# A ten-buffer gather, spills on GpSimd and ScalarE one-hots in the U stage of a hybrid decoder layer; norms that scale the rows

## The reference, cut to what matters

```
q   = (h @ wq).reshape(B, S, 8, 2, 128)
sub = einsum("bshpd,hpnd->bshpn", q, keys)
sv, si = top_k(sub, 16)                      # per half, then 16 of the 16*16 sums
experts, gates = ids of the best 16, softmax(best)
act = gelu(einsum("cd,ced->ce", xb, u_tab[experts]))   # 128 experts a token
out = einsum("ce,ced->cd", gates * act, v_tab[experts])
x = rms_norm(x + out)
```

## Time and profile before

| | us |
|---|---|
| runs, median | 1961.11 |
| lowest, highest of three | 1956.55, 1967.15 |
| profiled execution, its own time | 1952.49 |
| its span, first to last instruction | 1950.7 |
| TensorE busy | 1862.3 (95%) |
| VectorE, ScalarE, GpSimd busy | 1580.6, 1031.1, 783.9 |

### The profile page before, as it was taken

How to read it: one execution, slowest core, us unless ns; L and a number is a source line. 1 busy time by engine, 2 the same in 40 slices (tenths; PEclk the granted TensorE clock), 3 DMA queues, 4 the chain that set the end, 5 groups by cost and what they waited for, 6 DMA issues and landing times.

```text
span 1950.7 us, 34571 instructions
## 1 busy us (share of the span) xinstructions
PE 1862.3 (95%) x13106; PEld 1628.1 (83%) x13106; DVE 1580.6 (81%) x2510; ACT 1031.1 (53%) x1868; POOL 783.9 (40%) x686
## 2 busy tenths in 40 slices
PE   8999999999999999999998989988999999999997
PEld 7888887787889888788887877868999999998886
DVE  6768575676534999899987878878988999999998
ACT  5535454474555454666745656535674444444444
POOL 0000000000011113677635677004776777787773
PEclk9999999999999999999999999999999999999999
DMA  7523333246799997888868989977979999999997
GB/s 251 190 86 131 99 99 109 78 133 226 251 302 310 315 321 221 248 265 268 250 216 279 317 283 314 317 249 258 314 246 372 380 387 383 383 393 392 396 382 265
DMA packets 214741, 520.70 MB, mean 267 GB/s; under 512 B 25424, under 2 KB 98416, under 8 KB 214320
## 3 DMA queue, kind: packets, MB, share of 16 engines
q1 hardware_dynamic: 171952, 356.41, 52.9%
q0 software_dynamic: 42624, 162.08, 24.3%
HBM read 472.18 MB, written 46.20 MB: 266 GB/s over the span
## 4 chain that ended last, share of the span: by engine, by line
PE 60%; DMA 14%; DVE 14%; ACT 5%; issue 4%; POOL 3%; SPq 0%; DVEq 0%; ACTq 0%; POOLq 0%
PE ps L2043 59%; DVE lo L1330 4%; DMA raw<-in_peer_u 3%; DMA vraw<-in_peer_v 3%; DMA oneJ_spill<-hspace 2%; DMA hspace<-u_rows,row_ids 1%; POOL u_early L789 1%; PE ps L2447 1%; DMA u_late<-u_rows,row_ids 1%; ACT hi L870 1%; DMA u_early<-u_rows,row_ids 1%; POOL hspace L789 1%; POOL u_late L789 1%; DVE hspace L1862 1%; DMA oneI<-oneI_spill 1%
## 5 line engine op out<-in xcount | busy, mean ns | idle before, releaser
L2043 PE MATMUL ps<-hT,hi 128*128 128x512 f32 x2736 | 990.4, 405 | 39.1 <-DVE lo L1330 38.8
L2043 PE MATMUL ps<-hT,lo 128*128 128x256 f32 x2736 | 769.1, 281 | 0.0
L2043 PEld LDWEIGHTS ps<-hT,hi 128*128 128x128 f32 x2736 | 517.6, 189 | 176.3 <-issue 33.7
L870 ACT ACTIVATE hi<-raw 128x896 fp32r<-128x896 f32 (+1 forms) x406 | 397.2, 991 | 363.8 <-DMA raw<-in_peer_u 303.5
L1330 DVE TENSOR_TENSOR lo<-raw,hi 128x896 fp32r<-128x896 f32 (+1 forms) x406 | 457.6, 1139 | 126.8 <-ACT hi L870 122.5
L2043 PEld LDWEIGHTS ps<-hT,lo 128*128 128x128 f32 x2736 | 520.4, 190 | 0.1
L827 POOL DMA_INDIRECT got<-in_peer_v,row_ids x256 | 345.9, 1351 | 121.9 <-DVE sums L1338 100.9
L1203 ACT ACTIVATE vhi<-vraw 128x896 fp32r<-128x896 f32 (+1 forms) x256 | 193.6, 765 | 255.4 <-DMA vraw<-in_peer_v 247.7
L2043 PE MATMUL ps<-vhi,a_hi 128*128 128x448 f32 x768 | 242.0, 370 | 7.3 <-DVE vlo L1894 5.6
L1338 DVE SCALAR_TENSOR_TENSOR sums<-got,wT,sums 128x704 f32<-128x704 f32 x256 | 243.0, 949 | 1.4 <-DMA got<-in_peer_v,row_ids 0.9
L2043 PE MATMUL ps<-vlo,a_hi 128*128 128x448 f32 x768 | 241.0, 368 | 0.0
(11 more groups left out here) (314 smaller groups left out, 2257.2 us busy)
## 6 DMA issues: line engine op xcount, KB each, us to landing
raw<-in_peer_u SPq DMA_DIRECT2D x256, 448.0 KB, 4.8
vraw<-in_peer_v SPq DMA_DIRECT2D x124, 448.0 KB, 7.9
raw<-in_w_in SPq DMA_DIRECT2D x86, 512.0 KB, 3.4
vraw<-in_peer_v SPq DMA_DIRECT2D x124, 224.0 KB, 8.0
raw<-in_w_out SPq DMA_DIRECT2D x32, 512.0 KB, 3.8
raw<-in_wq SPq DMA_DIRECT2D x32, 512.0 KB, 5.3
turn_in<-in_peer_u SPq DMA_DIRECT2D x32, 512.0 KB, 5.9
u_rows<-turned POOLq DMA_DIRECT2D x32, 512.0 KB, 5.7
```

The costliest lines, as they stand in the source:

```text
L870: nc.scalar.activation(hi[n % NR][:, 0:w], raw[n % NR][:, 0:w], ACT.Copy).then_inc(hi_done, 1)
L2043: return nc.tensor.matmul(o, lhsT, rhs, start=start, stop=stop, skip_group_check=True)
```

## The change

It consists of these parts.

- Gathered rows: ten buffers in each half (`u_space`: `h0`, `h1` and `e0` to `e7` first, then `l0` to `l3` and `m0` to `m3`, six in all for dots from tile 98 on, four from tile 107 on). `u_buffers` gives each pair its buffer and the pair that had it before. GpSimd waits for the dot (not the sum) of pair k - 6, for the sum of the pair before in the same buffer, and at a first use of an `m` buffer for ScalarE's copies of both `idx` banks.
- Sums: ScalarE sums a dot three pieces behind it (`SUM_LAG`), after the single hi piece.
- Spills: they leave SyncE's queue. GpSimd takes gathers and spills from one order, `pool_order`: a gather of k is keyed by the dot of k - 6 plus 0.6 piece, a spill by its one-hot plus 0.7. The last ones, from `U_LATE`, follow in their order.
- Late one-hots: they begin when the last dot is done, and every second J part is made by ScalarE (`late_j`) as 1 - |j - number| through Abs, four times 128x128, and Relu, 128x512, in one buffer `tail4`. It waits for the landing of the spill two before. VectorE still makes all I parts and the other J parts, with `hspace`.
- The plan: pace 0.92 for 0.87, a late J of ScalarE costs half, the last dot has to stand before tile 113.
- Norms: VectorE scales the rows themselves, four tensor_scalar of 128x512 a half (`rows_scaled`), and TensorE transposes them. In the second norm the additions of the second half are moved among the steps of the first half's factor.
- `w65_ready` and `scan_done` become one semaphore.

What `u_plan` and `pool_order` give (positions as tile, .5 is its second piece):

| | before | after |
|---|---|---|
| room | 1.28 | 1.24 |
| row numbers of the halves | 24.0, 70.0 | 25.0, 72.5 |
| dots 0, 60, 64, 127 | 26.0, 61.5, 72.0, 109.5 | 27.0, 63.5, 74.5, 112.5 |
| idx copied by ScalarE in iteration | 74 | 76 |
| one-hots 0, 31, 63 | 75.0, 107.0, 126.5 | 77.0, 110.5, 126.0 |
| `U_LATE`, its place | 47, 117.5 | 34, 113.5 |
| spills ahead of gather 127 in GpSimd's order | 0 | 30 (0 to 29) |

The diff, without renamed lines and without what only moves:

```diff
@@ u_plan
-        pace = min(pace + 0.87, 2.0)
+        pace = min(pace + 0.92, 2.0)
...
-                ones, credit = ones + 1, credit - ONE_US
+                if late is None and dots == N_PAIR and n > last_dot + 1:
+                    late = ones
+                by_act = late is not None and (ones - late) % 2
+                ones, credit = ones + 1, credit - (ONE_US / 2 if by_act else ONE_US)
...
-    if _done:
+    if _done and LAST_DOT < 2 * (T_U + 113):
@@
+def pool_order():
+    order, key = [], 0.0
+    for k in range(N_PAIR):
+        key = max(key, ROWS_AT[k * NT2 // N_PAIR], DOT_AT[k - U_BUF] + 0.6 if k >= U_BUF else 0)
+        order.append((key, k, "gather"))
+    order += [(ONE_AT[g] + 0.7, g, "spill") for g in range(U_LATE)]
+    return sorted(order)
@@ sync: spill(g) and its calls removed
@@ gpsimd
+            def spill(g):
+                split = g >= U_LATE and (g - U_LATE) % 2 == 0
+                if g < U_LATE or split:
+                    pool.wait_ge(sem("madeJ"), g + 1 if g < U_LATE else U_LATE + (g - U_LATE) // 2 + 1)
+                else:
+                    pool.wait_ge(sem("lateJ_made"), (g - U_LATE) // 2 + 2)
+                pool.dma_start(oneJ_dram[g]..., made_j(g)).then_inc(sem(f"oneJ_out{g % 3}"), 16)
+                pool.wait_ge(sem("madeI"), g + 1)
+                pool.dma_start(oneI_dram[g]..., made_i(g)).then_inc(sem(f"oneI_out{g % 2}"), 16)
@@ gather of pair k
                 if k >= U_BUF:
-                    pool.wait_ge(sem("dots_summed"), k - U_BUF + 1)
+                    pool.wait_ge(sem("dots_made"), k - U_BUF + 1)
+                if U_PREV[k] is not None:
+                    pool.wait_ge(sem("dots_summed"), U_PREV[k] + 1)
+                elif U_HOME[k][0] == "m":
+                    for i in range(2):
+                        wait_read(pool, "idx", i)
@@ scalar
+            def late_j(g):
+                act.wait_ge(sem("p_made"), 1)
+                if g == U_LATE + 1:
+                    act.wait_ge(sem("dots_summed"), N_PAIR)
+                    act.wait_ge(sem("lateJ_made"), 1)
+                else:
+                    act.wait_ge(sem(f"oneJ_out{(g - 2) % 3}"), 16 * ((g - 2) // 3 + 1))
+                for c in range(TOK4):
+                    at_c = TOK4 * (g - U_LATE) + c
+                    ins = nc.scalar.activation(made_j(g)[:, c], iota[:, :], ACT.Abs,
+                                               bias=minus_j[:, at_c:at_c + 1])
+                ins.then_inc(sem("far_made"), 1)
+                act.wait_ge(sem("far_made"), (g - U_LATE) // 2 + 1)
+                nc.scalar.activation(made_j(g), made_j(g), ACT.Relu, scale=-1.0, bias=one_c).then_inc(
+                    sem("lateJ_made"), 1)
...
+                for n in range(2 * (T_U + i) + 2, 2 * (T_U + i) + 4):
+                    if n < 2 * T_V:
+                        hi_piece(n)
+                    for what, k in U_STEPS.get(n - SUM_LAG, []):
+                        if what == "dot":
+                            dots_sum(k)
+                    for what, g in U_STEPS.get(n - 1, []):
+                        if what == "one" and g >= U_LATE and (g - U_LATE) % 2:
+                            late_j(g)
@@ vector, first norm
-                ts(diag[t][:, :], ident[:, :], rs[:, t:t + 1], None, ALU.mult).then_inc(
-                    sem("diag_done"), 1)
+                for q in range(4):
+                    rows = x_sb[:, t, 512 * q:512 * q + 512]
+                    ts(rows, rows, rs[:, t:t + 1], None, ALU.mult).then_inc(sem("rows_scaled"), 1)
@@ vector, second norm
-            add_rows(0, range(4))
-            norm_rows(0)
-            add_rows(1, range(4))
-            norm_rows(1)
+            add_rows(0, range(4))
+            add_rows(1, range(1))
+            norm_sum(0)
+            add_rows(1, range(1, 2))
+            norm_factor(0)
+            add_rows(1, range(2, 4))
+            scale_rows(0)
+            norm_sum(1)
+            norm_factor(1)
+            scale_rows(1)
@@ tensor, first norm (second alike)
-                        ins = mm(bank("x1", j)[...], x_sb[:, t, kc * P:(kc + 1) * P], diag[t][:, :], ...)
+                        ins = nc.tensor.transpose(bank("x1", j)[...],
+                                                  x_sb[:, t, kc * P:(kc + 1) * P], ident[:, :])
```

More of the change, by code:

```diff
@@ L150, with u_buffers @@
     U_STEPS, _done, (U_EXP, U_FIRST, LAST_DOT, ROWS_AT) = u_plan(_room / 100)
-    if _done:
+    if _done and LAST_DOT < 2 * (T_U + 113):
         break
[L153 to L157, removed]
 ONE_AT = {_i: _n for _n in U_STEPS for _what, _i in U_STEPS[_n] if _what == "one"}
-U_LATE = min([_i for _i, _n in ONE_AT.items() if _n >= 2 * (T_U + 117)] + [SEQ // 4])
+DOT_AT = {_i: _n for _n in U_STEPS for _what, _i in U_STEPS[_n] if _what == "dot"}
+U_LATE = min([_i for _i, _n in ONE_AT.items() if _n > LAST_DOT + 1] + [SEQ // 4])
 U_PDOT = LAST_DOT // 2 - T_U + 3
+N_LATE_ACT = (SEQ // 4 - U_LATE) // 2
+SUM_LAG = 3
+def u_buffers():
+    homes, prev, last, half = {}, {}, {}, N_PAIR // 2
+    turn = [0, 0, 0]
+    for k in range(N_PAIR):
+        if k < half:
+            home = (["h0", "h1"] + [f"e{i}" for i in range(8)])[turn[0] % 10]
+            turn[0] += 1
+        elif DOT_AT[k] < 2 * (T_U + 98):
+            home = (["h0", "h1"] + [f"l{i}" for i in range(4)] + [f"m{i}" for i in range(4)])[turn[1] % 10]
+            turn[1] += 1
+        else:
+            late = DOT_AT[k] >= 2 * (T_U + 107)
+            home = (["h0", "h1", "l2", "l3"] + ([] if late else ["l0", "l1"]))[turn[2] % (4 if late else 6)]
+            turn[2] += 1
+        homes[k], prev[k] = home, last.get(home)
+        last[home] = k
+    return homes, prev
+U_HOME, U_PREV = u_buffers()
+def pool_order():
+    order, key = [], 0.0
+    for k in range(N_PAIR):
+        key = max(key, ROWS_AT[k * NT2 // N_PAIR], DOT_AT[k - U_BUF] + 0.6 if k >= U_BUF else 0)
+        order.append((key, k, "gather"))
+    order += [(ONE_AT[g] + 0.7, g, "spill") for g in range(U_LATE)]
+    return sorted(order)
 DD = 1344
@@ L452, in u_got @@
         def u_got(k):
[L454 to L457, removed]
+            home = U_HOME[k]
+            if home[0] == "h":
+                return hspace[:, int(home[1]), 7:KC:8, :]
+            return u_space[home][:, :, :]
         def made_j(g):
@@ L643, in _ @@
                         raw_in[n % NR], 16)
-                    if n - 3 in U_STEPS:
-                        for what, g in U_STEPS[n - 3]:
-                            if what == "one":
-                                spill(g)
                 if t + 1 in U_TURN:
@@ L651, in _ @@
                     load_unit(N_Q)
-            for n in range(2 * T_V - 3, 2 * T_V):
-                for what, g in U_STEPS[n]:
-                    if what == "one":
-                        spill(g)
             def load_v(k):
@@ L793, in _ @@
                         sem(f"got_in{k % U_BUF}"), 16)
+            for _, i, what in pool_order():
+                if what == "gather":
+                    gather_rows(i)
+                else:
+                    spill(i)
+            for g in range(U_LATE, N_TOK4):
+                spill(g)
             def cast_rows(c):
@@ L1194, in _ @@
                         freed("idx", 1), 1)
+                    act.wait_ge(freed("idx", 1), PLAN["idx", 1][1] + 1)
+                    nc.scalar.activation(minus_j[:, :], idxT[:, 1, TOK4 * U_LATE:SEQ], ACT.Copy,
+                                         scale=-1.0).then_inc(sem("lateJ_made"), 1)
             def v_hi(k):
```

96 lines of the change are left out of this document (39 added, 57 removed).

## The result

The changed kernel takes 2002.51 us (median of 4 runs, 1995.82 to 2009.70) where the kernel before takes 1959.86 beside it: ratio 1.0198, 95% interval 1.0150 to 1.0245. I had forecast 1968, with a range to 1985: the time lies outside it. The profiled execution took 1995.8 us, with a span of 1994.0 where before has 1950.7; 43.3 us are to be explained, where my sum has 7.

What follows compares the result with a forecast made beforehand. TensorE, busy 95% of the span, was taken as the bound, so changes pay only where it starves. First dots -8.5, second dots +7, tail +8.5 and norms 0 gave 7 us slower: 1968 us, range 1945 to 1985.

Steps and rivals of the forecast that it cites:

- my sum: Whole kernel: the four steps added up, 7 us slower; chance 0.40, own range 1959 to 1975 us.
- Norms, nothing: Both norms: row scaling by VectorE and transposes by TensorE change the time by 0 us.
- First dots, -8.5: First dots of the U stage: GpSimd's waits for sums go, 8.5 of 10.5 us lost are gained.
- Second dots, +7: Second dots of the U stage: spills on GpSimd's queue make it set the pace, 7 us more lost.
- 198 us to spill 29: Second dots: GpSimd's time for 56 pairs and 30 spills before issuing spill 29, which VectorE's one-hot 31 awaits.
- Tail, +8.5: Tail of the U stage: ScalarE waits for J spills to land, 19.6 us lost for 11.1.
- The round: Tail: ScalarE's four Abs, Relu and wait for its J spill's landing, 5.5 us, fourteen times.
- Cheap gathers: Rival, dots: gather issues fall to a mean of about 1.0 us, kernel faster at 1943 us; chance 0.22.
- A J landing of 2.5 or of 4.3: Two rivals, tail: spill lands in 2.5 us, total 1960, chance 0.14; or in 4.3, total 1985, chance 0.14.
- Cold transposes: Rival, norms: transposes don't bring TensorE's doubled pace, so products start at half pace, 1974 us; chance 0.08.
- The chance of 0.30 for slower: Whole kernel: probability given to a result more than 0.5% slower; faster had 0.27, within 0.5% 0.43.
- Theory G: Experiments' forecasts, first dots: unbroken trains of gathers keep TensorE short of instructions; four pairs open saves 4 to 10 us.

Runs made afterwards that it cites:

- 10: Changed kernel with at most four pairs of gathers open instead of six; ratio 1.0122 to the kernel before.
- run 11: Changed kernel with spills issued by SyncE and at most four pairs of gathers open; ratio 0.9925 to the kernel before.
- run 4: Changed kernel with all late J parts made by VectorE, spills still by GpSimd; ratio 1.0216 to the kernel before.
- 8: Changed kernel with four I buffers instead of two until dot 127; ratio 1.0106 to the kernel before.
- 15: Changed kernel with four I buffers and at most four pairs of gathers open; ratio 1.0118 to the kernel before.
- run 1: Kernel before with the norms' edit alone; ratio 0.9988 to the kernel before.
- 2: Changed kernel with spills back on SyncE and all late J parts by VectorE, six pairs open; ratio 1.0006 to the kernel before.
- 5: Changed kernel with spills back on SyncE, all late J parts by VectorE and four pairs open; ratio 0.9905 to the kernel before.

## Why the prediction was wrong, step by step

**Norms, nothing.** Right. One reading was not: the 1.00 that the view prints for the clock from 8 to 10 us is no record, since the trace of before has none ahead of 13.0 us.

**First dots, -8.5: the step that failed most, by 21 us.** Its working (GpSimd fast enough, waits for sums gone, dots 3.0 us apart, 2 us left) is what runs 10 and 11 show, with 1.2 and -0.2 us lost. What it left out is a way in which TensorE starves that no term had: once TensorE fell behind, GpSimd, freed of its waits, went on with gathers to the limit of six, and TensorE stayed slow until it stopped. Eleven traces have five or more weight loads close together with gaps of over 0.4 us and no semaphore; in eight of them the last comes 1.4 to 2.9 us behind the last gather's end before a pause, in 4 an isolated one 1.0 us behind it, in 8 and 15 the last is 1.5 and 2.4 us ahead of it. That the waits which I booked as pure loss had also been a brake fits this, but is argued: run 1 has the waits and a short stall too. Traces of ten buffers with six or eight pairs open have 15 to 34 us lost in this stretch, those with three or four 0 to 16, so single traces overlap. What is shown is the limit's worth by time: 1.0% without spills on GpSimd (2 to 5) and 0.8% with them (change to 10), in both dots stages together. I had also read GpSimd's waits for sums too small, from one group of two: they were 13.8 us in the first dots for 11.6 and 36.7 in the second for 30.8.

**Second dots, +7: too small by 18.** The bound was named rightly: GpSimd without a break. Its 198 us to spill 29, from 1046.4 on, would end at 1244.4; that J spill went out at 1261.0. Of the 16.6 us, 9 are waits for sums near the end, most in the last nine pairs, which have four buffers (ACT hspace 7.6, ACT u_l 1.0), where I had put 1.5 at most. Some 5 are the dearer gathers (114 times 0.04), and 3 one pair more than I counted. Further, the wait of 12.6 us at 1062.5 is an order I had not followed: I had costed what the spills take from the gathers, not what gathers in front of a spill take from VectorE, which has two I buffers. Four I buffers or four open pairs give 7 to 10 us of the stretch back in the traces.

**Tail, +8.5: too small by 7, with only part of the blame right.** The round was under-priced: 6.4 us for 5.5, since the J spill was released 3.9 us behind its issue and not 3.1. Fourteen rounds took 89.3 us where I had 77. But with all late J parts on VectorE (run 4) the tail still loses 20.6, and the whole time is no shorter. Of the 15.6 us more than before, 6 go with ScalarE's part and 10 with GpSimd issuing the spills, whoever makes the J part, which my sum had only as ScalarE's landing. VectorE there waits 13.8 us for J spills and 3.0 for I spills; in the changed kernel ScalarE waits 35.0 for J and VectorE 28.5 for I. From SyncE (run 11) the same tail loses 15.7, with 10.4 us of waits on ScalarE.

**The rivals.** Cheap gathers: false, 1.205 us at the mean. A J landing of 2.5 or of 4.3: neither, 3.9 at the mean, nearer the slow one. Cold transposes: there in ten of sixteen traces, for 1.5 us and not in the changed kernel's own. The chance of 0.30 for slower was too low: each rival priced one known place, and none the stall, of which the trace of before shows next to nothing.

**The clock.** The mean grant is 0.978, with 0.992 before; it falls behind each stall (0.50 from 840 to 848 us) and isn't in my sum. What it costs by itself I could not separate, since TensorE was starved in the same stretches.

**Open.** What TensorE waits for in the stall. No semaphore, no clock and no DMA share (0.56, under the 0.86 before it) explains it. Theory G's shortage of instructions isn't shown: TensorE's are fetched in packets of 16 KB, some 250 instructions, and in the trace with eight open the packets around the stall start at 814.8 and 853.4 us, while it ends at 833 between them. What sets it off, between 790 and 850 us, is not shown either: at 800 us 1 to 2.5 pairs are open with six allowed, 2 with four. That the limit helps is measured; by which resource, not.

## What to carry to other kernels

A queue's wait may be a brake that something else needs: if buffers are added to remove it, set how far the engine may run ahead as a number of its own, and try it smaller than the buffers allow (0.9905 with four of ten here, 1.0006 with six). When DMAs move to another in-order queue, cost both directions, what they delay and what stands ahead of them, and compare the queue's whole occupancy with the stage: GpSimd had 15 us free in 185, and the spills took 36. Undo one part at a time from the changed kernel: one of its parts carried four fifths of the loss, and the others, with a limit, made a kernel that is 0.95% faster than the one before.

## What was not expected of the hardware

TensorE's weight loads, without a wait that the profile names, came 0.7 us apart for some 20 us at a granted clock that was 1.00 at first, while gathers went on at 1.25 us each; it ended some 2 us behind the last gather ahead of GpSimd's pause. During 32 float32 transposes TensorE's pace doubled in eleven traces of sixteen (from 0.21 us apart to 0.11), and in six of these it halved again for 3.4 us behind a pause of 2.4 us, so that products took 0.63 and 0.41 us and then 0.40 and 0.28.
